# A two-layer hybrid transformer kernel: the projections of one attention moved between the head-norm steps of the other

## The reference, cut to what matters

```
h = rms_norm(x, g_norm1) * (1 + sc1) + sh1
u = h @ w_in + b_in
q_lat, kv_lat, k_rope, q_sb, k_sb, v_sb, gate_mla, gate_sb = split(u)   # 256,128,64,512,512,512,1024,1024

q  = rms_norm(q_lat) @ w_uq           # 4 heads of 128 + 64 (rope)
kv = rms_norm(kv_lat) @ w_ukv         # 4 heads of 128 (key) + 128 (value)
k  = concat(k_nope, k_rope for every head)
q, k = rms_norm over each head's 192, then rope on the last 64
y_mla = causal_softmax_attention(q, k, v_mla)

z = q_sb k_sb^T / sqrt(128);  l = log_sigmoid(-z) where key < query, else 0
y_sb = (exp(z + reverse_cumsum_keys(l)) where key < query) @ v_sb

merged = sigmoid(gate_mla) * (y_mla @ w_branch_mla) + sigmoid(gate_sb) * (y_sb @ w_branch_sb)
x = x + gt1 * (merged @ w_out)        # then norm, up projection, conv, down projection
```

## Time and profile before

| | us |
|---|---|
| median of 3 runs | 4050.49 |
| lowest, highest | 4039.59, 4065.84 |
| span of the profiled execution | 4045.2 |
| TensorE busy (89% of the span) | 3587.1 |
| VectorE busy (31%) | 1237.5 |
| ScalarE busy (18%) | 743.2 |
| layer 1, first matmul of the latents to first matmul of merge | 1867.86 to 2231.91 |
| mean granted TensorE clock over the span | 0.899 |

### The profile page before, as it was taken

One profiled execution on the slowest core, in us unless ns is written; L12 is line 12 of the kernel. 1 busy time (PEld: TensorE's weight loads), 2 busy tenths in 40 slices (PEclk: granted clock), 3 DMA queues, 4 the chain that ended last, 5 costly groups with the idle time before them and its releaser, 6 DMA issues.

```text
span 4045.2 us, 33392 instructions
## 1 busy us (share of the span) xinstructions
PE 3587.1 (89%) x12783; PEld 2015.6 (50%) x12783; DVE 1237.5 (31%) x2193; ACT 743.2 (18%) x1290; POOL 139.7 (3%) x192
## 2 busy tenths in 40 slices
PE   5899788888797899987877899999998788999999
PEld 3365388884344777863433344444434233444444
DVE  3434356555576111112123002332012220123310
ACT  2221322221001111112242111110012311111100
POOL 0000000000010111111000000000000000000000
PEclk7857889999898999998976999999998769999999
DMA  5100000005773999982100111222211001122220
GB/s 188 63 0 33 30 1 1 1 1 187 270 275 123 308 355 350 356 297 95 55 21 0 63 63 62 72 74 78 75 55 42 21 0 63 68 75 65 83 78 37
DMA packets 232682, 413.24 MB, mean 102 GB/s; under 512 B 8177, under 2 KB 137757, under 8 KB 232429
## 3 DMA queue, kind: packets, MB, share of 16 engines
q1 hardware_dynamic: 204800, 314.59, 22.5%
q0 software_dynamic: 27232, 95.51, 6.5%
q10 hardware_dynamic: 525, 1.46, 0.1%
HBM read 386.34 MB, written 25.19 MB: 102 GB/s over the span
## 4 chain that ended last, share of the span: by engine, by line
PE 80%; DVE 8%; DMA 5%; issue 3%; ACT 3%; POOL 0%; ACTq 0%; POOLq 0%; DVEq 0%; SPq 0%
PE PS L431 44%; PE PS L1973 7%; PE PS L1449 5%; PE PS L935 3%; PE PS L1457 3%; DMA AR<-idx_rows 2%; PE PS L638 2%; PE PS L1657 1%; PE PS L657 1%; PE PS L401 1%; PE PS L964 1%; DMA AR<-hn_rows,AR 1%; PE PS L1860 1%; PE PS L1859 1%; DVE TMP L410 1%
## 5 line engine op out<-in xcount | busy, mean ns | idle before, releaser
L431 PE MATMUL PS<-HN,W 128*128 128x512 f32 x2880 | 1270.3, 603 | 65.6 <-DMA W<-in_w_branch_sb 24.5
L431 PEld LDWEIGHTS PS<-HN,W 128*128 128x128 f32 x2880 | 552.5, 193 | 773.4 <-issue 738.1
L431 PE MATMUL PS<-AR,W 128*128 128x512 f32 (+1 forms) x784 | 356.5, 609 | 20.6 <-DVE AR L1764 11.8
L1973 PE MATMUL PS<-AR,W 128*128 128x512 f32 x704 | 302.5, 592 | 0.0
L1449 PE MATMUL PS<-AR,W 128*128 128x128 f32 x2560 | 291.3, 276 | 8.0 <-DVE AR L1490 8.0
L1449 PEld LDWEIGHTS PS<-AR,W 128*128 128x128 f32 x2560 | 288.2, 192 | 11.4 <-issue 11.3
L431 PEld LDWEIGHTS PS<-AR,W 128*128 128x128 f32 (+1 forms) x784 | 150.2, 193 | 215.4 <-issue 215.4
L1973 PEld LDWEIGHTS PS<-AR,W 128*128 128x128 f32 x704 | 133.8, 190 | 168.4 <-issue 168.4
L1951 DVE TENSOR_SCALAR AR<-AR,VEC 128x512 f32<-128x512 f32 x88 | 42.9, 488 | 390.9 <-ACT AR L1931 390.9
L509 DVE TENSOR_TENSOR H<-H,TMP 128x512 f32<-128x512 f32 x40 | 27.7, 692 | 413.2 <-ACT TMP L494 413.2
L1931 ACT ACTIVATE AR<-PS 128x512 f32<-128x512 f32 x88 | 52.6, 598 | 534.2 <-PE PS L431 534.2
(11 more groups left out here) (445 smaller groups left out, 3710.3 us busy)
## 6 DMA issues: line engine op xcount, KB each, us to landing
W<-in_w_up SPq DMA_DIRECT2D x84, 1024.0 KB
W<-in_w_in SPq DMA_DIRECT2D x26, 2048.0 KB
AR<-in_w_ada POOLq DMA_DIRECT2D x24, 2048.0 KB, 8.8
W<-in_w_gate SPq DMA_DIRECT2D x40, 1024.0 KB
W<-in_w_down SPq DMA_DIRECT2D x40, 1024.0 KB
y_rows<-AR SPq DMA_DIRECT2D x40, 512.0 KB, 11.0
AR<-in_ada_w POOLq DMA_DIRECT2D x8, 2048.0 KB, 8.4
W<-in_w_down SPq DMA_DIRECT2D x8, 2048.0 KB
```

What stands on the lines that cost most here:

```text
L431: mm = pe.matmul(o, l, r, start=(i == 0), stop=(i == len(products) - 1))
L1973: mm = pe.matmul(PS[g % 4][:, :], w[:, k - k0, m * P:(m + 1) * P], FF[:, k, :], start=(k == 0), stop=(k == FT - 1))
```

## The change

The order of the calls becomes: latents' projection, `latent`, first SB group, `heads_proj`, `heads_norm` with the other 11 SB groups issued product by product between its steps, `sb`, `mla`, `merge`. Weights follow: block 14 is now that of `heads_proj`, 15 and 16 those of SB keys and values. The tiles of the SB attention are packed (only the causal part is stored, 1280 words instead of 2048), and AR is laid out anew so that the finished MLA queries, keys and values stay while SB runs. `merge` in the layers gets its own places for MG and YT. In `latent` and `heads_norm`, ScalarE now does Ln and Exp of one tile in turn, after one preload of a table that has both.

```diff
+        def group_steps(pe, g, it, products, tiles_ready=None):
...
                 mm = pe.matmul(o, l, r, start=(i == 0), stop=(i == len(products) - 1))
-            mm.then_inc(proj_done, 1)
-            return mm
+                if i == len(products) - 1:
+                    mm.then_inc(proj_done, 1)
+                yield i
...
-        GL = {"lat": 0, "qsb": 4, "ksb": 8, "vsb": 12, "qn": 16, "qr": 20, "kn": 24, "vm": 28, "merge": 32, "out": 64,
-              "up": 72, "down": 116}
+        GL = {"lat": 0, "qn": 5, "qr": 9, "kn": 13, "vm": 17, "merge": 32, "out": 64, "up": 72, "down": 116}
+        BESIDE = 6
+
+        def sbg(i):
+
+            return 4 if i == 0 else 20 + i
...
+        def sb_proj_steps(pe, L):
+            it, gi = (L, L_BLOCKS), (L, L_GROUPS)
+            for i in range(12):
+                m, n = i % 4, LB + (13, 15, 16)[i // 4]
+                if m == 0:
+                    arrived(pe, n, it)
+                if i < 8:
+                    yield from group_steps(pe, LG + sbg(i), gi, channel_products(slot(n), m, HN))
+                else:
+                    if m == 0:
+                        pe.wait_ge(row_in, L * 16 + 16)
+                    yield from group_steps(pe, LG + sbg(i), gi, token_products(slot(n), m, HN) + [(ones[0:1, :], ROW)])
+
+        def sb_taken_by(matmuls):
+
+            ends = [8 * (i + 1) + max(0, i - 7) for i in range(12)]
+            return sum(e <= matmuls + 8 for e in ends)
...
-            pe.wait_ge(proj_taken, L * L_GROUPS + (LG + 16))
+            pe.wait_ge(proj_taken, L * L_GROUPS + (LG + GL["merge"]))
+            pe.wait_ge(hd_done, L * 8 + 8)
             scores(0)
...
+            act.preload_act_table_set("natural_log_exp_and_others")
             for x, n in ((0, 256), (1, 128)):
                 act.wait_ge(lat_ss, L * 2 + (x + 1))
                 own(act.activation(TMP[:, x, :], PS[4 + x][:, :], ACT.Ln, scale=1.0 / n, bias=EPSC[:, 0:1]))
-            for x in range(2):
                 act.activation(TMP[:, x, :], TMP[:, x, :], ACT.Exp, scale=-0.5).then_inc(lat_r, 1)
...
         def heads_norm_act(act, own, L):
...
+            taken = 1
+            for i in range(2 * MH):
+                act.wait_ge(hd_ss, L * 8 + (i + 1))
+                if i >= 2:
+                    act.wait_ge(hd_n, L * 8 + (i - 1))
+                own(act.activation(TMP[:, i % 2, :], PS[4 + i % 2][:, :], ACT.Ln, scale=1.0 / (NOPE + ROPE), bias=EPSC[:, 0:1]))
+                act.activation(TMP[:, i % 2, :], TMP[:, i % 2, :], ACT.Exp, scale=-0.5).then_inc(hd_r, 1)
+                while taken < sb_taken_by(2 * BESIDE * (i + 1)):
+                    sb_proj_act(act, L, taken)
+                    taken += 1
...
                 pe.matmul(PS[4 + i % 2][:, :], ones[0:ROPE, :], HEADSQ[0:ROPE, i % 2, 1, :], start=False, stop=True).then_inc(hd_ss, 1)
+                for _ in range(BESIDE):
+                    next(beside, None)
                 if i >= 1:
                     rotate(i - 1)
+                for _ in range(BESIDE):
+                    next(beside, None)
             rotate(2 * MH - 1)
+            for _ in beside:
+                pass
...
-                attn_proj_pe(pe, L)
+                lat_proj_pe(pe, L)
+                latent_pe(pe, L)
+                sb_proj = sb_proj_steps(pe, L)
+                for _ in range(8):
+                    next(sb_proj)
+                heads_proj_pe(pe, L)
+                heads_norm_pe(pe, L, sb_proj)
                 sb_pe(pe, L)
-                latent_pe(pe, L)
-                heads_proj_pe(pe, L)
-                heads_norm_pe(pe, L)
                 mla_pe(pe, L)
```

More of the change, by code:

```diff
@@ L431, in group @@
                 mm = pe.matmul(o, l, r, start=(i == 0), stop=(i == len(products) - 1))
-            mm.then_inc(proj_done, 1)
-            return mm
+                if i == len(products) - 1:
+                    mm.then_inc(proj_done, 1)
+                yield i
+        def group(pe, g, it, products, tiles_ready=None):
+            for _ in group_steps(pe, g, it, products, tiles_ready):
+                pass
         def take(act, g, it):
@@ L515, in out_pe @@
                 for m in range(4):
-                    group(pe, g0 + 4 * hf + m, gi, channel_products(slot(n0 + hf), m, YT))
+                    group(pe, g0 + 4 * hf + m, gi, channel_products(slot(n0 + hf), m, YT[int(it is not None)]))
                     if beside:
@@ L1633, in attn_proj_act, with sb_proj_act @@
                 act.activation(dst[m], take(act, LG + m, gi)[0:n, :], ACT.Identity, bias=vec("b_lat", m)[0:n]).then_inc(proj_taken, 1)
[L1634 to L1641, removed]
+        def sb_proj_steps(pe, L):
[13 more added lines that the diff above has]
+            return sum(e <= matmuls + 8 for e in ends)
+        def sb_proj_act(act, L, i):
+            b = take(act, LG + sbg(i), (L, L_GROUPS))
+            m = i % 4
+            if i < 4:
+                act.activation(QSB[:, m, :], b[:, :], ACT.Identity, scale=SB_SCALE, bias=SMB[:, m:m + 1]).then_inc(proj_taken, 1)
+            elif i < 8:
+                act.activation(KSB[:, m, :], b[:, :], ACT.Identity, bias=vec("b_ksb", m)).then_inc(proj_taken, 1)
+            else:
+                act.activation(VSB[:, m, :], b[:, :], ACT.Copy).then_inc(proj_taken, 1)
         def sb_pe(pe, L):
@@ L1793, in heads_norm_act, with heads_norm_pe @@
         def heads_norm_act(act, own, L):
-            for pair in range(0, 2 * MH, 2):
-                for i in (pair, pair + 1):
-                    act.wait_ge(hd_ss, L * 8 + (i + 1))
-                    if i >= 2:
-                        act.wait_ge(hd_n, L * 8 + (i - 1))
-                    own(act.activation(TMP[:, i % 2, :], PS[4 + i % 2][:, :], ACT.Ln, scale=1.0 / (NOPE + ROPE), bias=EPSC[:, 0:1]))
-                for i in (pair, pair + 1):
-                    act.activation(TMP[:, i % 2, :], TMP[:, i % 2, :], ACT.Exp, scale=-0.5).then_inc(hd_r, 1)
-        def heads_norm_pe(pe, L):
+            taken = 1
[8 more added lines that the diff above has]
+                    taken += 1
+            while taken < 12:
+                sb_proj_act(act, L, taken)
+                taken += 1
+        def heads_norm_pe(pe, L, beside):
             def rotate(i):
```

98 lines of the change are left out of this document (46 added, 52 removed).

## The result

The changed kernel takes **3944.6 us** (median of 4 runs, 3929.5 to 3950.7), the kernel before 4045.5 us (median of 4, 4039.6 to 4065.8). The ratio is **0.974, 95% interval 0.972 to 0.977**: 2.6% faster. The profiled execution has a span of 3927.8 us; the sum had said 3929, and 3934 for the median. It is itself the fastest of the four, so the median stands 17 us above it, not 5.

What follows compares the result with a forecast made beforehand. TensorE's projection products carry most of the chain, while the head norms run at clock 0.56 waiting for VectorE and ScalarE. Savings of 50.1 + 1.9 + 6 = 58.0 us a layer, 116 in two, gave 3934 us; range 3893 to 3974.

Steps and rivals of the forecast that it cites:

- the sum: All three terms: 58.0 us less a layer, 116 us in two, giving a span of 3929 and a median of 3934 us.
- Part 1: SB products go under the head norms: latents' norm, heads_proj and head norms 141.1 us against 191.2, 50.1 less a layer.
- block 16 that nobody waits for: SB values' weights, loaded 24 products into the head norms, cost nothing; upward bound 12.4 us if the load starts late.
- does not overlap: Rival: waits in head norms' steps serialise own chain and products, 68 + 80 us; 4014 us in all, chance 0.03.
- Part 2: SB attention: no table loads, two loads on the path save 2.6 us, 0.7 added; 1.9 us less a layer.
- further drain: SB table loads: the Trainium skill's extra 1.38 us per switch would gain 2.8 us more a layer; trace disagreed.
- Part 3: MLA attention: entered at full clock behind SB's dense products, its first period gains; 6 us less a layer.
- I take the present pattern: MLA periods after the first: assumed to keep the clocks they had in the kernel before, so no further gain.
- clock holds through MLA: Rival: MLA runs at full clock throughout, 18 instead of 6 us less a layer; 3910 us, chance 0.25.
- Merge's wait: Merge's wait for its weights by DMA, with TensorE idle: stays unchanged at 12.4 us.
- Isolated pace: Rival: the 92 SB products beside the head norms take 1.05 us instead of 0.874; 3966 us, chance 0.10.
- clock stays low: Rival: head norms with products keep 1.2 GHz, 209 us instead of 107.8; 4137 us, slower, chance 0.02.

Runs made afterwards that it cites:

- tables, old order: The kernel before with one preload of the table holding both Ln and Exp ahead of the SB attention, nothing moved: 4043.9 us, ratio 0.999.
- unpaired, old order: The kernel before with the one table preload and the head norms' Ln and Exp head by head instead of in pairs: 4008.9 us, ratio 0.990.
- none beside: The changed kernel with no SB products between the head norms' steps; the 92 products follow behind the last rotation: 3972.6 us, ratio 0.982.
- three beside: The changed kernel with 3 SB products in each place of the head norms instead of 6, 44 behind the last rotation: 3934.8 us, ratio 0.972.
- this kernel's 3909 us: The changed kernel with 3 products in each place of the head norms and two unread products in each MLA gap: 3909.2 us, ratio 0.966.

## Why the prediction was right, step by step

**Part 1: size right, reasons only in part.** It said 141.1 us for latents' norm, heads_proj and the stretch; measured are 11.8 + 20.9 + 109.5 = 142.2. Each of the three terms is within 2 us. The step time, the cover of the own chain and of sixteen loads (run without the preload), the clock of 0.99 and a block 16 that nobody waits for all came as written. But it put the whole gain down to products going *under* the norms. Before, the part took 191.2 us; the runs split the 49 like this, per layer:

| step | from | us |
|---|---|---|
| table loads | 191.2 to 183.4 (tables, old order) | 7.8 |
| Ln and Exp head by head | to 168.2 (unpaired, old order) | 15.2 |
| new place: norm of the latents covered, heads_proj at full clock | to 159.4 (none beside) | 8.8 |
| products beside the head norms | to 142.2 (changed) | 17.2 (15.8 in layer 2) |

The sum did not need this split, since it replaced the old stage by a bound on TensorE. It would have needed it for the rival "does not overlap". That was priced with the old stage's own 68 us, 68 + 80, giving 4014 us. The run without overlap has 43.8 + 82.9 and gave 3972.6. What its price left out is above all that the heads are no longer paired: an edit with a worth of its own, 15 us, that I had not priced. It also left in the 5 us of table loads of the head norms. And the 8.5 us that I read as the chain of a step held the waits of the pairs: head by head a step takes 46 / 8 = 5.8 us.

**Part 2: mis-sized.** Forecast -1.9 us, measured +0.6 (64.0 to 64.6). The stage gained 3.2 in the old order, 2.6 of them in the two waits. The step that failed is the start of the stage. I had noted the 2.2 us of idleness ahead of it, but costed the scores behind it at the 4.58 us of the earlier trace rows, which followed dense products. They took 7.30. With products in front of them (three beside) the stage is 62.4, within 0.3 of what the prediction had. The further drain that was weighed there shows nowhere: with four loads off their path the head norms gained 5.1 us, 1.28 each, and the two waits in SB fell by 1.3 us each.

**Part 3: right for the profiled execution.** 78.7 to 72.5, forecast 73, with the first period gaining the 6 us. Its ground was weaker than the text said: "I take the present pattern" has no cause behind it, and the repeat of the same kernel had 78.5 in one layer. The same code took 71 to 90 us in seven kernels. In the four layers profiled of the changed kernel it took 71.4 to 78.5, so the term could have come out 6 us longer in each layer. That it hit is in part luck. The rival "clock holds through MLA" did not happen here, but its price was about right: at 0.97 MLA took 58.7 us, where the rival has 60.7. That this kernel's 3909 us is also the rival's 3910 is chance, since it holds the gain of three beside as well. The Trainium skill (TensorE: Matmul & The Clock Gate, "Part 4: PE-mode transpose") says that a transpose does not count as TensorE work for the clock gate as other products do. No run here isolates this: the same transposes stood in every MLA, at 0.56 and at 0.97, and only the dense products beside them were varied.

**The rest.** Merge's wait stayed within 1 us. The sum was 1 us above the profiled span, and this closeness is luck: the terms gave 110.7 us in two layers and not 116, and 6.7 us came from stages that the sum left alone. The median stands 17 us over that span where I had carried over 5, so the forecast came out 11 us low. The 5 us rested on three runs; with the fourth the kernel before has a median of 4045.5, and the change took off 101 us where I had 116. "Isolated pace" is refuted by 5.42 us for 12 records, 0.90 us a product; "clock stays low" by 0.99.

## What to carry to other kernels

Before a stage's gain is credited to overlap, run or price the stage with the other edits alone: here about a third of the projections' and norms' 49 us a layer came from overlap, and a third from splitting a pairing of two activations that no longer had a reason once one table set held both. A stage with short products and waits between them can be TensorE-bound at the half clock, and then what helps is dense work put between its products, even work that nobody reads: price it by the low-clock busy time (41 us) against the same products at full clock (25). Look at the stage behind as well: its clock can change though its code does not, and of 11 us gained in front of one, 7.7 disappeared in it.

## What the runs showed of the hardware

- The same 16 score records took 4.58 us behind dense products and, after 2.30 us of idleness, from 5.93 to 7.52 us (7.30 in the changed kernel's layer 1).
- One code at one place, MLA, took 72 and 78 us in the two layers of a single execution, with the clock at 0.74 and 0.67 and every other engine's time equal.
- Eight unread products (16 records) in a stage of 168 records shortened it from 78.7 to 64.2 us in the old order, and from 72.5 to 58.6 us with three products beside.
- A table load cost 1283 ns and no further drain: 5.1 us for four on the path, and sixteen of them cost nothing under a busy TensorE.
